# An expert loop of fp32 weights split in two halves: where VectorE makes the gate-up product among the low halves

## The reference

```
D_FF_EXPERT = 3584; N_EXPERTS = 8; TOP_K = 2; D_MODEL = 1024; SEQ = 256

def swiglu(h, w_gate, w_up, w_down):
    return (jax.nn.silu(h @ w_gate) * (h @ w_up)) @ w_down

def moe_swiglu(h, w_router, w_gate, w_up, w_down):
    logits = (h @ w_router).astype(jnp.float32)
    top_vals, top_idx = lax.top_k(logits, TOP_K)
    top_w = jax.nn.softmax(top_vals, axis=-1)
    combine = jnp.einsum('bsk,bske->bse', top_w,
                         jax.nn.one_hot(top_idx, N_EXPERTS, dtype=jnp.float32)).astype(h.dtype)
    out = jnp.zeros_like(h)
    for e in range(N_EXPERTS):
        out = out + combine[..., e:e + 1] * swiglu(h, w_gate[e], w_up[e], w_down[e])
    return out
```

## Time and profile before

| what | value |
|---|---|
| median of 3 runs | 1955.95 us (1951.67 to 1956.32) |
| span of the profiled execution | 1948.8 us |
| TensorE busy (matmuls) | 1814.7 us, 93% |
| VectorE busy | 1499.8 us, 77% |
| ScalarE busy | 1185.8 us, 61% |
| weights read | 456 granules of 1 MB, 251 GB/s over the span |
| one expert (from the first transpose of `turn(6)` to that of the next) | 129.63 us |

### The profile page before, as it was taken

One profiled execution on the slowest core, in us unless ns is written; L12 is line 12 of the kernel. 1 busy time (PEld: TensorE's weight loads), 2 busy tenths in 40 slices (PEclk: granted clock), 3 DMA queues, 4 the chain that ended last, 5 costly groups with the idle time before them and its releaser, 6 DMA issues.

```text
span 1948.8 us, 27555 instructions
## 1 busy us (share of the span) xinstructions
PE 1814.7 (93%) x10676; PEld 1599.8 (82%) x10676; DVE 1499.8 (77%) x1506; ACT 1185.8 (61%) x1181; POOL 114.3 (6%) x107
## 2 busy tenths in 40 slices
PE   7887899997799998778999999999999999999996
PEld 7777899997799997677878878878788788787885
DVE  7888788857666556646888888878788888887886
ACT  5434477743344444536767767767677777676774
POOL 1000145401100000010000000000000000000000
PEclk9988999998899998887999999999999999999998
DMA  7423354693355545124998989979889799798893
GB/s 293 152 96 115 122 188 175 202 251 130 118 181 178 195 176 214 65 76 168 371 344 311 371 296 363 370 290 369 342 320 370 299 359 369 293 366 336 326 366 127
DMA packets 68622, 489.89 MB, mean 251 GB/s; under 512 B 7552, under 2 KB 7936, under 8 KB 10048
## 3 DMA queue, kind: packets, MB, share of 16 engines
q1 hardware_dynamic: 66528, 480.89, 66.0%
q0 software_dynamic: 2016, 7.92, 2.0%
HBM read 484.58 MB, written 4.19 MB: 251 GB/s over the span
## 4 chain that ended last, share of the span: by engine, by line
PE 72%; DVE 16%; ACT 7%; issue 4%; DMA 0%; POOL 0%; DVEq 0%; ACTq 0%; SPq 0%; POOLq 0%
PE psum L617 22%; PE psum L619 22%; PE psum L618 22%; DVE wlo L1387 7%; ACT whi L1024 3%; PE psum L888 2%; DVE acc L1499 2%; ACT whi L1318 2%; PE psum L939 1%; DVE xtm L1926 1%; DVE al L1428 1%; ACT L1318 0%; ACT s L1241 0%; DMA par<-params 0%; PE psum L667 0%
## 5 line engine op out<-in xcount | busy, mean ns | idle before, releaser
L1387 DVE TENSOR_TENSOR wlo<-wraw,whi 128x2048 fp32r<-128x2048 f32 x456 | 1042.4, 2290 | 297.5 <-ACT whi L1318 165.8
L1318 ACT ACTIVATE whi<-wraw 128x2048 fp32r<-128x2048 f32 x336 | 643.3, 1919 | 270.4 <-PE psum L619 269.6
L617 PE MATMUL psum<-whi,xgh 128*128 128x512 f32 x896 | 359.1, 401 | 5.0 <-DVEq L1918 4.4
L617 PE MATMUL psum<-ah,whi 128*128 128x256 f32 x1176 | 345.2, 294 | 19.0 <-DVE al L1428 11.4
L618 PE MATMUL psum<-wlo,xgh 128*128 128x512 f32 x896 | 354.0, 395 | 0.0
L619 PE MATMUL psum<-whi,xgl 128*128 128x512 f32 x896 | 353.9, 395 | 0.0
L618 PE MATMUL psum<-al,whi 128*128 128x256 f32 x1176 | 338.3, 288 | 0.0
L619 PE MATMUL psum<-ah,wlo 128*128 128x256 f32 x1176 | 337.8, 287 | 0.0
L1024 ACT ACTIVATE whi<-wraw 128x2048 fp32r<-128x2048 f32 x118 | 225.1, 1909 | 149.1 <-PE psum L619 145.2
L617 PEld LDWEIGHTS psum<-ah,whi 128*128 128x128 f32 x1176 | 231.6, 197 | 22.3 <-issue 10.6
L618 PEld LDWEIGHTS psum<-al,whi 128*128 128x128 f32 x1176 | 231.7, 197 | 0.7
(11 more groups left out here) (332 smaller groups left out, 2260.4 us busy)
## 6 DMA issues: line engine op xcount, KB each, us to landing
wraw<-weights SPq DMA_DIRECT2D x456, 1024.0 KB, 4.9
bias_rows<-ttab POOLq DMA_DIRECT2D x1, 3072.0 KB, 35.3
btab<-bias_rows POOLq DMA_DIRECT2D x1, 2048.0 KB, 11.5
xres<-x SPq DMA_DIRECT2D x1, 1024.0 KB, 7.1
btab<-bias_rows POOLq DMA_DIRECT2D x1, 1024.0 KB, 13.9
out<-outb SPq DMA_DIRECT2D x2, 512.0 KB, 2.7
recip<-recip_counts POOLq DMA_DIRECT2D x1, 512.0 KB, 4.9
fgain<-final_gain POOLq DMA_DIRECT2D x1, 512.0 KB, 3.4
```

Source lines behind the costliest of these rows:

```text
L617: nc.tensor.matmul(out, lh, rh, start=start, stop=False)
L1318: sc.activation(whi[:, g % NS, :], wraw[:, g % NW, :], ACT.Copy).then_inc(hi_done, 1)
L1387: return ve.tensor_tensor(dst, value, hi.bitcast(f32), SUB)
```

## The change

In `expert` of VectorE the product of the next chunk, issued in step ("D", c, 0) for c from 0 to 5, stands ahead of the low half of granule j+2 instead of behind it. The product of chunk 0 (j = 4) stays where it is.

```diff
                 for j, (kind, c, half) in enumerate(MOE):
                     g = GD + j + 2
+                    if kind == "D" and half == 0 and c < FC - 1:
+                        product(c + 1)
                     v.wait_ge(hi_done, E * BODY + (g + 1))
                     lo(wlo[:, g % NS, :], wraw[:, g % NW, :], whi[:, g % NS, :]).then_inc(lo_done, 1)
                     if kind == "U" and half == 0 and c:
                         turned(c - 1)
-                    if (kind == "D" and half == 0 and c < FC - 1) or j == 4:
-                        product(c + 1 if kind == "D" else 0)
+                    if j == 4:
+                        product(0)
                     if kind == "D" and c == FC - 3 and half == 1:
                         v.wait_ge(sct_done, E + 1)
                         select(E + 1)
```

## The result

The changed kernel is slower, not a little faster: 1965.3 us (median of 13 runs, 1958.88 to 1992.03) against 1954.34 us (13 runs), a ratio of 1.0056 with a 95% interval of 1.0036 to 1.0077. The ratio leaves out the two slowest of the 13, of 1990.33 and 1992.03 us, and the profiled execution is the slowest of all: it shows in all 8 experts what the others, by their times, have in some.

What follows compares the result with a forecast made beforehand. TensorE was taken to set the loop's pace, but for one 2.2 us transpose wait an expert. A gain of 0.56 less 0.08 us, eight times 0.48, is 3.8 us: 1955.95 to 1952.1 us, range 1947 to 1957 us.

Steps and rivals of the forecast that it cites:

- The product and the stall: At an expert's end, the transposes' 2.2 us wait for the product becomes some 1.8 us at the gather for `atl`.
- The gain: At the gather, it starts 0.56 us earlier less 0.08 us: 0.48 us for an expert, 3.8 us over eight.
- The cost of the start after a stall: In the gather, slow first matmuls behind the wait take back 0.08 us, between nothing and 0.15 us.
- The other 40 products: On VectorE, products not at an expert's end gain and cost nothing; the low half behind has 1.05 us to spare.
- The stall of 2.16 us leaves the clock at 1.00, and the new one is shorter: On TensorE at the gather, the argument against a lower clock: the old transpose stall left it at 2.4 GHz.
- The rival: At the gather, the moved stall halves TensorE's clock ahead of short matmuls: 9.5 us slower, 1965.4 us; chance 0.03.
- The price of a fall: At the gather, eight matmuls at the halved clock cost 1.66 us each time, 13.3 us over the experts.
- the idle 4.38 us: Ahead of the loop, TensorE's idle stretch, with 8 matmuls at clock 0.50 behind it, said to agree with the skill's rule.
- The whole stall: At an expert's end, the rival that all 2.41 us is won: 19.3 us, 1936.7 us; chance 0.06.

Runs made afterwards that it cites:

- the second run of 1: Kernel before with only the products of chunks 1 to 5 moved ahead of the low halves, chunk 6's left behind: 1953.78 us, ratio 1.0009.
- 5: Kernel before, no product moved, with one unused VectorE maximum ahead of the low half of the turned product: 1976.2 us, ratio 1.0112.
- the idle matmuls of 4: Changed kernel with seven unused 512-column matmuls between the gather's wait and the gather: 1959.54 us, ratio 1.0034.
- The two kernels without a stall: Changed kernel: first, gather's `at_lo` wait put behind its 32 matmuls, 1930.51 us; second, turned product's copies put ahead of D61's halves, 1930.14 us.

## Why the prediction was wrong

**The product and the stall: right.** The transposes' waits went, 8 waits of the gather for `atl` came, 1.8 us each. `atl` ends where it was forecast, within 0.02 us in relation to D50.

**The gain, 0.48 us for an expert: right in kind, too large by a fifth.** Experts without a fall take 129.25 us, so it is 0.38 us and 3.0 us in all. The gather starts 0.14 us behind the end of `atl` (1148.85 + 0.68 = 1149.53, then 1149.67), not 0.06 us as the transposes do behind the product. The cost of the start after a stall, 0.08 us, was about right: the gather starts 0.46 us earlier and 0.38 us of it are left. The upper bound of that cost, 0.79 less 0.63 us, is 0.16 us and not 0.15, which changes nothing here.

**The other 40 products cost nothing: right.** Moved alone they give 1.0009, with an interval that holds 1; in the changed kernel TensorE waits for low halves as often as before (7 times, 3.8 against 3.7 us).

**"The stall of 2.16 us leaves the clock at 1.00, and the new one is shorter": this step failed.** It took the length of the stall for what decides, and one execution without a fall for the rule. In the kernel before the stall stands between two down granules of full-width matmuls, with four transposes at its end; the changed kernel puts it ahead of the gather, 32 matmuls of 128 columns. A stall of 1.8 us there brought the clock down in three of eight experts in one profiled execution and in all eight in another, and 1.1 us did so in three. The same length of stall with full-width matmuls behind it gives two short falls or none. And the stall of 2.2 us at its old place isn't safe either: it has no fall in the profiled execution of before, but two of 3.4 us in that of the second run of 1, and four in that of 5. The rival was named, and got 0.03.

**The price of a fall: too low.** I took 1.66 us, from the 3.5 us of matmuls that ran at the lower clock behind the idle stretch ahead of the loop. Those rows were misread as well: in the kernel before the clock was down already over the 19 us ahead of that idle stretch, so the idle time didn't bring it down, and the 3.5 us are only the end of a longer fall. The stretch ahead, and the idle one:

```profile
869.50:888.90 19.40, 14.32 (x64) 13.45 (x64) 10.21 (x24) 3.58 (x7) 0.00 (x0) 0.50 0.13 52
888.90:893.28 4.38, 0.00 (x1) 0.01 (x1) 0.95 (x6) 4.29 (x6) 0.00 (x0) 0.50 0.00 0
```

Beside the gather the clock stays down for 10.2 us of solid work in most falls, which at half the clock costs about half of it: 4.8 us as measured (3.2 us for the shortest fall, 6.4 us for the longest). The excess of the median over before, 1965.3 - 1954.34 = 11.0 us, with the gain of 3.0 us that it hides, would be three falls of 4.8 us, an estimate. The profiled execution had eight. That the rival's 1965.4 us is almost the time measured is luck: it charged 1.66 us in all eight experts, too little for each of too many.

The prediction set against its rows what the Trainium skill says ("TensorE: Matmul & The Clock Gate", part 1): the clock halves after idleness and returns only behind sustained work. The trace agrees in that the stall was paid twice, with 1.8 us of idle time and 4.8 us at the lower clock. The agreement that it saw for the idle 4.38 us rests on the rows misread above. And idleness alone doesn't tell when: the same stall ahead of the idle matmuls of 4 brought no fall.

**The whole stall** (19.3 us): right for what it is worth, and the order of the changed kernel does not win it. The two kernels without a stall are 21 and 23 us below before by their ratios (1.09% and 1.16% of 1954 us), with the 127.2 us for an expert that the prediction named; eight times the difference of an expert (129.63 less 127.2 us) is 19.4 us.

## What to carry to other kernels

When a stall of TensorE only moves, look at what it moves next to: ahead of narrow matmuls a stall shorter than one that mostly did no harm elsewhere can bring the clock down, and the price was then two to three and a half times the stall (3.2 to 6.4 us for 1.8 us). Look at more than one execution before calling a stall harmless. Follow the chain behind a removed wait to the next one, and remove both: here either edit alone gave nothing or a loss, and the pair 1.1%. If a stall can't be removed, keep it apart from narrow matmuls, or fill it.

## What the runs showed of the hardware

The falls are not the same in every execution of one program. The run with only the last product moved had three in eight experts; the changed kernel's profiled execution had eight, and its 13 runs spread over 33 us, from 1958.88 to 1992.03. The kernels without a stall keep within 5 and 7 us, and that spread isn't of the loop: the slowest run of the second (1936.07 us, profiled) and a usual one of the first (1930.52 us, profiled) both have experts of 127.2 us, but the first gather of the loop starts at 1016.9 us in the one and at 1012.5 us in the other.

The falls of the stall ahead of the transposes, in the run with only the other products moved: in two of its experts the clock was down behind it; one such stretch, its expert, and the expert after it:

```profile
1140.20:1143.80 3.60, 3.34 (x11) 2.81 (x12) 3.00 (x3) 0.60 (x2) 0.00 (x0) 0.53 0.97 380
...
1014.10:1145.20 131.10, 128.81 (x584) 104.78 (x583) 109.49 (x66) 93.34 (x65) 0.00 (x0) 0.99 0.88 336
1145.20:1274.80 129.60, 127.27 (x583) 103.62 (x582) 109.50 (x66) 93.35 (x65) 0.00 (x0) 1.00 0.89 336
```

Such a fall costs 1.5 us. It may be part of why the runs of before spread over 9 us (1950.2 to 1959.07), beside what varies ahead of the loop; that was not tried. Which execution gets how many falls, when after a stall they set in, and why a fall beside the gather lasts longer than one beside full-width matmuls, stays open.
